# Attention values of the sampled stage: from split fp32r products on 128 weight columns to plain fp32 products on 32 weight columns in four strips

## The reference

```python
def sample_attn(q, k, v, lam, k_past, v_past, rel_bias):
    ...
    s_past = diff_logits(q, q_pos, k_past, jnp.arange(past, dtype=jnp.int32), rel_bias)
    s_new = diff_logits(q, q_pos, k, q_pos, rel_bias)
    w = diff_weights(jnp.concatenate([s_past, s_new], axis=-1), lam).astype(v.dtype)
    return (jnp.einsum('bhqk,bkhe->bqhe', w[..., :past], v_past)
            + jnp.einsum('bhqk,bkhe->bqhe', w[..., past:], v))
```

## Time and profile before

| | |
|---|---|
| median of 3 runs | 2045.65 us (2044.92 to 2045.75) |
| profiled execution, first to last instruction | 2043.6 us |
| difference of the two | 2.05 us |
| TensorE matmul busy | 1993.2 us (98% of the span) |
| VectorE / ScalarE / GpSimd busy | 1375.8 / 998.2 / 131.7 us |
| sampled stage, turns 0 to 8 | about 835 to 1077 us |
| one turn in its middle | 27.5 us |

### The profile page before, as it was taken

The page is one execution under the profiler, slowest core; times in us unless marked ns, Lnnn a source line. Parts: engine busy times, 40 slices in busy tenths (PEclk is TensorE's granted clock), DMA queues, the critical chain, the costliest instruction groups (busy, mean ns, idle before and its releaser), DMA issues. The chain is left out here.

```text
span 2043.6 us, 36009 instructions
## 1 busy us (share of the span) xinstructions
PE 1993.2 (98%) x11888; PEld 1850.2 (91%) x11888; DVE 1375.8 (67%) x2932; ACT 998.2 (49%) x1770; POOL 131.7 (6%) x158
## 2 busy tenths in 40 slices
PE   6999999999999999799999999999999999999998
PEld 6999999999999999688878799999999998989896
DVE  6766776767676767678785376675757474847476
ACT  5756575757565757677874242222313141313133
POOL 0000000000000000145560000000000000000000
PEclk9999999999999999999999999999999999999999
DMA  6411111112121112788873131111112020202012
GB/s 199 144 57 54 57 53 56 53 60 59 50 59 50 59 52 87 261 306 304 316 268 92 38 93 42 53 42 42 52 32 62 22 72 22 72 21 69 6 53 99
DMA packets 167453, 183.26 MB, mean 90 GB/s; under 512 B 11045, under 2 KB 139589, under 8 KB 167349
## 3 DMA queue, kind: packets, MB, share of 16 engines
q1 hardware_dynamic: 166137, 181.24, 27.1%
q10 hardware_dynamic: 1212, 0.81, 0.1%
HBM read 162.82 MB, written 24.46 MB: 92 GB/s over the span
## 5 line engine op out<-in xcount | busy, mean ns | idle before, releaser
L1250 PE MATMUL ps<-h_hi,w_hi 128*128 128x384 f32 (+1 forms) x1152 | 386.7, 336 | 5.0 <-DVEq L967 3.4
L1250 PE MATMUL ps<-h_hi,w_lo 128*128 128x384 f32 (+1 forms) x1152 | 376.5, 327 | 0.0
L1250 PE MATMUL ps<-h_lo,w_hi 128*128 128x384 f32 (+1 forms) x1152 | 376.4, 327 | 0.0
L2456 PE MATMUL ps<-h_hi,f_w_hi 128*128 128x320 f32 (+1 forms) x1136 | 370.7, 326 | 0.8 <-PEq L1579 0.8
L2456 PE MATMUL ps<-h_hi,f_w_lo 128*128 128x320 f32 (+1 forms) x1136 | 370.4, 326 | 0.0
L2456 PE MATMUL ps<-h_lo,f_w_hi 128*128 128x320 f32 (+1 forms) x1136 | 370.2, 326 | 0.0
L2535 ACT ACTIVATE yc<-ps,f_prm 128x384 f32<-128x384 f32 x144 | 93.5, 653 | 560.6 <-PE ps L2456 400.0
L2436 PE MATMUL ps<-d_hi,act 128*128 128x512 f32 x816 | 257.0, 390 | 0.5 <-issue 0.5
L1250 PEld LDWEIGHTS ps<-h_hi,w_hi 128*128 128x128 f32 x1152 | 217.0, 188 | 9.0 <-issue 4.0
L1250 PEld LDWEIGHTS ps<-h_lo,w_hi 128*128 128x128 f32 x1152 | 217.1, 188 | 0.6
L1250 PEld LDWEIGHTS ps<-h_hi,w_lo 128*128 128x128 f32 x1152 | 216.8, 188 | 0.0
(11 more groups left out here) (310 smaller groups left out, 3525.2 us busy)
## 6 DMA issues: line engine op xcount, KB each, us to landing
k<-in_cache_k SPq DMA_DIRECT2D x64, 512.0 KB, 5.9
v_raw<-in_cache_v SPq DMA_DIRECT2D x64, 512.0 KB, 4.7
w_raw<-in_w_in SPq DMA_DIRECT2D x48, 512.0 KB, 4.0
f_raw<-in_w_up SPq DMA_DIRECT2D x48, 512.0 KB, 4.0
f_raw<-in_w_down SPq DMA_DIRECT2D x24, 512.0 KB, 3.5
bias<-bias_tiles_dram SPq DMA_DIRECT2D x8, 576.0 KB, 3.6
merged_dram<-mg SPq DMA_DIRECT2D x8, 544.0 KB, 2.7
ow_raw<-in_w_out SPq DMA_DIRECT2D x8, 512.0 KB, 7.5
```

Source lines behind the costliest of these rows:

```text
L1250: last_ = pe.matmul(bank(s)[:, 0:n], w[:, W_SLOT[g], k, :], x[:, k, off:off + n], start=(k == 0 and i == 0), stop=(k == KT - 1 and i == 2))
L2456: l_ = pe.matmul(ps[:, e % 6, 0:n], w[:, p, k, :], x[:, k, off:off + n], start=(k == 0 and i == 0), stop=(k == KT - 1 and i == 2))
```

## The change

Values and transposed weights are no longer split in the sampled stage. `pt_sb` holds the transposed weights once, in fp32, 64 columns for each page. The matmuls of a page take `v_raw` directly: the half hf of the value columns (heads 4 hf to 4 hf + 3) against the 32 weight columns of these four heads, in plain fp32. The result goes to one of four strips of 32 PSUM partitions of one bank: strip 2 hf + n % 2. The two strips of a half hold the even and the odd pages and are added in the fold. `o2` is one bank instead of two, so `o2s`, the copy and the transposes are half as large. A page waits for its load alone. All splits of value pages, of the new rows and of the transposed weights are gone from ScalarE, VectorE and GpSimd.

```diff
-SPLIT_AT = {2: (0, 1), 3: (2,), 4: (3,), 5: (4, 5), 6: (6,), 7: (7,)}
...
-    o2 = ps[:, 6:8, :].rearrange("p a n -> p (a n)")
-    ptn = ps[:, 6, 0:NS]
+    o2 = ps[:, 6, :]
+    ptn = ps[:, 7, 0:NS]
...
-    pt_both = sb("pt_both", [128, NPAGES + 1, 2, NS], F32R, 158784)
-    o2s = sb("o2s", [128, D], F32, 163392)
+    pt_sb = sb("pt_sb", [128, NPAGES + 1, NS], F32, 158784)
+    o2s = sb("o2s", [128, 512], F32, 163392)
...
+    def strip(hf, n):
+
+        q = 2 * hf + n % 2
+        return o2[32 * q:32 * q + 32, :]
...
-    own_rows = bass.AP(tensor=o2.tensor, offset=o2.offset,
-                       ap=[o2.ap[0], [128 + DEC_T, H], [1, DEC_T], [NS, 2]])
+    def own_rows(hf):
+
+        return bass.AP(tensor=o2.tensor, offset=o2.offset + 64 * hf,
+                       ap=[o2.ap[0], [128 + DEC_T, HH], [1, DEC_T], [32, 2]])
...
-                    if has(b, 1):
-                        for n in splits_of(b).get(h, ()):
-                            if n in POOL_PAGES:
-                                pool.wait_ge(vhi_done, 8 * (b - 1) + n + 1)
-                                pool.tensor_tensor(v_lo[:, n, :], v_raw[:, n, :], v_hi[:, n, :].bitcast(F32),
-                                                   ALU.subtract).then_inc(vplo_done, 1)
...
-                for g in range(H):
+                for g in range(HH):
                     last = pe.transpose(o2[:, 128 * g:128 * (g + 1)], o2s[:, 128 * g:128 * (g + 1)], c.ident[:, :])
...
                 if n == NPAGES:
-                    pe.wait_ge(new_lo, 2)
-                elif n in POOL_PAGES:
-                    pe.wait_ge(vplo_done, pool_low(b, ("v", n)))
+                    pe.wait_ge(vn_in, 32)
                 else:
-                    pe.wait_ge(vlo_done, len(DVE_PAGES) * (b - 1) + DVE_PAGES.index(n) + 1)
+                    pe.wait_ge(v_in[n], 16 * b)
                 for hf in range(2):
                     cols = slice(512 * hf, 512 * (hf + 1))
-                    parts = (v_hi[:, n, cols], v_lo[:, n, cols]) if n < NPAGES else (vn[:, cols],)
-                    for x, v in enumerate(parts):
-                        last = pe.matmul(o2[:, cols], pt_both[:, n, :, :].rearrange("p a n -> p (a n)"), v,
-                                         start=(n == 0 and x == 0), stop=(n == NPAGES - 1 and x == 1))
+                    v = v_raw[:, n, cols] if n < NPAGES else vn_raw[:, cols]
+                    last = pe.matmul(strip(hf, n), pt_sb[:, n, 32 * hf:32 * hf + 32], v,
+                                     start=(n < 2), stop=(n in (NPAGES - 1, NPAGES)))
...
-                            pe.wait_ge(ptlo_done, 2 * b)
+                            pe.wait_ge(pthi_done, 2 * b)
...
-                    if has(b, 1):
-                        for n in splits_of(b).get(h, ()):
-                            act.wait_ge(v_in[n], 16 * b)
-                            act.activation(v_hi[:, n, :], v_raw[:, n, :], ACT.Copy).then_inc(vhi_done, 1)
...
-                    if h == 3 and has(b, 1):
-                        dve.wait_ge(pthi_done, 2 * b)
-                        dve.tensor_tensor(pt_lo[:, 0:NPAGES, :], pt.rearrange("p (n k) -> p n k", n=NPAGES),
-                                          pt_hi[:, 0:NPAGES, :].bitcast(F32), ALU.subtract).then_inc(ptlo_done, 1)
...
-                            dve.wait_ge(vhi_done, 8 * (b - 1) + n + 1)
-                            dve.tensor_tensor(v_lo[:, n, :], v_raw[:, n, :], v_hi[:, n, :].bitcast(F32),
-                                              ALU.subtract).then_inc(vlo_done, 1)
```

More of the change, by code:

```diff
@@ L1396 @@
 HH = H // 2
-SPLIT_AT = {2: (0, 1), 3: (2,), 4: (3,), 5: (4, 5), 6: (6,), 7: (7,)}
 PV_EARLY = {5: (2,)}
 PV_AT = {4: (0, 1), 5: (), 6: (3,), 7: (4,), 8: (5, 6, NPAGES)}
-POOL_PAGES = (1, 3, 5, 7)
-DVE_PAGES = tuple(n for n in range(NPAGES) if n not in POOL_PAGES)
 LAST = DEC_B - 1
-SPLIT_LAST = {1: (0,), 2: (1, 2), 3: (3, 4), 4: (5,), 5: (6,), 7: (7,)}
 OUT_SPLITS = [("m", 0), ("w", 0), ("w", 1), ("w", 2), ("w", 3), ("m", 1), ("w", 4), ("w", 5), ("w", 6), ("w", 7)]
@@ L1406 @@
 OUT_LOW = [x for x in OUT_SPLITS if x[0] == "m" or x[1] >= 4]
-POOL_LAST = [x for h in range(H + 1)
-             for x in [("v", n) for n in SPLIT_AT.get(h, ()) if n in POOL_PAGES]
-             + [x for x in OUT_AT.get(h, ()) if x not in OUT_LOW]]
+POOL_LOW = [x for h in range(H + 1) for x in OUT_AT.get(h, ()) if x not in OUT_LOW]
 def sampled_and_out(nc, sb, sem, ins, outs, c):
@@ L1418, in sampled_and_out @@
     pt = ps[:, 5, :]
-    o2 = ps[:, 6:8, :].rearrange("p a n -> p (a n)")
-    ptn = ps[:, 6, 0:NS]
-    v_hi = sb("sv_hi", [128, NPAGES, D], F32R, 0)
-    v_lo = sb("sv_lo", [128, NPAGES, D], F32R, 32768)
+    o2 = ps[:, 6, :]
+    ptn = ps[:, 7, 0:NS]
     v_raw = sb("v_raw", [128, NPAGES, D], F32, 32768)
@@ L1443, in sampled_and_out @@
     kt_hi, kt_lo = kt[:, 0, :, :], kt[:, 1, :, :]
-    vn = sb("vn", [128, D], F32R, 202752)
     kn = sb("kn", [128, 2, H, NS], F32R, 206848)
@@ L1447, in sampled_and_out @@
     st = c.o_st
-    pt_hi, pt_lo = pt_both[:, :, 0, :], pt_both[:, :, 1, :]
     new_w = P[:, PAST:NKEYS]
-    new_twice = bass.AP(tensor=new_w.tensor, offset=new_w.offset, ap=[new_w.ap[0], [0, 2], [1, DEC_T]])
+    def strip(hf, n):
+        q = 2 * hf + n % 2
+        return o2[32 * q:32 * q + 32, :]
     def strips(part, at):
@@ L1491, in sampled_and_out @@
     c_done = sem("c_done")
-    vhi_done = sem("s_vhi_done")
-    vlo_done = sem("s_vlo_done")
     vplo_done = sem("s_vplo_done")
@@ L1498, in sampled_and_out @@
     pthi_done = sem("pthi_done")
-    ptlo_done = sem("ptlo_done")
     page_done = sem("page_done")
@@ L1547, in bank_of, with pool_low @@
         return 3 if t == 0 else 0 if t % 2 else 2
[L1549 to L1559, removed]
+    def pool_low(what):
+        return POOL_LOW.index(what) + 1
     def all_turns(eng, body):
@@ L1602, in new_weights @@
                     pool.sem_inc(settled, 1)
-                    pool.tensor_copy(p_new[:, :, bass.ds(DEC_T * (b - 2), DEC_T)], zeros[:, :, :]).then_inc(s_fill, 1)
+                    pool.tensor_copy(p_new[:, 0, bass.ds(DEC_T * (b - 2), DEC_T)], zeros[:, 0, :]).then_inc(s_fill, 1)
                 pool.wait_ge(exp_done, b)
                 pool.sem_inc(settled, 1)
-                pool.tensor_copy(p_new[:, :, bass.ds(DEC_T * (b - 1), DEC_T)], new_twice).then_inc(s_fill, 1)
+                pool.tensor_copy(p_new[:, 0, bass.ds(DEC_T * (b - 1), DEC_T)], new_w).then_inc(s_fill, 1)
             def weights_low(h):
@@ L1824, in out_tile @@
                     if t == 0 and k < 4:
-                        pe.wait_ge(vplo_done, pool_low(LAST, ("w", k)))
+                        pe.wait_ge(vplo_done, pool_low(("w", k)))
                     elif t == 0:
@@ L1927, in body @@
                         act.wait_ge(pt_done, b)
-                        act.activation(pt_hi[:, 0:NPAGES, :], pt.rearrange("p (n k) -> p n k", n=NPAGES), ACT.Copy)\
+                        act.activation(pt_sb[:, 0:NPAGES, :], pt.rearrange("p (n k) -> p n k", n=NPAGES), ACT.Copy)\
                            .then_inc(pthi_done, 1)
-                        act.activation(pt_hi[:, NPAGES, :], ptn, ACT.Copy).then_inc(pthi_done, 1)
+                        act.activation(pt_sb[:, NPAGES, :], ptn, ACT.Copy).then_inc(pthi_done, 1)
                     if h == 0 and at_start(b):
@@ L1941, in body @@
                             queries(b + 1, 0)
-                    if h == HH + 1 and isinstance(b, int) and b == 1:
-                        act.wait_ge(vn_in, 32)
-                        act.activation(vn[:, :], vn_raw[:, :], ACT.Copy).then_inc(new_hi, 1)
                     if h == 1 and has(b, 2):
@@ L2056, in fold_rows @@
                 dve.wait_ge(ot_done, b + 1)
-                dve.reduce_sum(oT[:, :, bass.ds(DEC_T * b, DEC_T)], own_rows, mybir.AxisListType.X)                   .then_inc(ots_done, 1)
+                for hf in range(2):
+                    last = dve.reduce_sum(oT[:, HH * hf:HH * (hf + 1), bass.ds(DEC_T * b, DEC_T)], own_rows(hf),
+                                          mybir.AxisListType.X)
+                last.then_inc(ots_done, 1)
             def split_out(what, i):
@@ L2082, in body @@
                         keys(b, h)
-                    if h == 3 and has(b, 1):
-                        dve.wait_ge(pthi_done, 2 * b)
-                        dve.tensor_tensor(pt_lo[:, 0:NPAGES, :], pt.rearrange("p (n k) -> p n k", n=NPAGES),
-                                          pt_hi[:, 0:NPAGES, :].bitcast(F32), ALU.subtract).then_inc(ptlo_done, 1)
-                        dve.tensor_tensor(pt_lo[:, NPAGES, :], ptn, pt_hi[:, NPAGES, :].bitcast(F32),
-                                          ALU.subtract).then_inc(ptlo_done, 1)
                     if at_start(b) and h == 0:
@@ L2096, in body @@
                         queries(b, HH)
[L2097 to L2100, removed]
                     if h == HH and has(b, 0):
@@ L2728 @@
```

(4 more changed lines are left out.)

## The result

The changed kernel takes 2022.15 us, the kernel before 2045.29 us in the same comparison. (The 2022.15 is the median of four runs: 2020.24, 2021.65, 2022.65 and one of 4954.44 us that stands alone; the median of the other three is 2021.65.) The ratio is 0.9882, 95% interval 0.9866 to 0.9898: 23 us faster. I had forecast 2058 us and slower, with 2018 to 2108 us as the range. The rival "four at once" had 2020 us.

The account below looks back on a forecast made before the run. TensorE's stream, busy 98%, was taken as the bound. A turn: 2.19 + 1.0 - 0.97 = +2.2 us, seven +15.5; with +0.2 - 3.0 - 0.3, +12.4 on 2045.65 gave 2058 us, range 2018 to 2108.

Parts of the forecast that it names:

- four at once: Rival: value matmuls in the four strips run free of each other; -2.6 us a turn, 2020 us; chance 0.27.
- What bounds it: Whole kernel: TensorE, busy 98% of the span, is nearly the bound; its idle time in five middle turns is for `kt_lo`.
- The cost of a record: Value matmuls: each plain fp32 matmul of 512 columns is two trace records of 0.44 us, 0.88 us in all.
- the groups of 4, 2, 2, 2 and 8: A turn's adjacent value matmuls: pages 0 and 1; page 2; page 3; page 4; pages 5, 6, new rows, 7.
- part 1: Value matmuls: m adjacent ones take (m + 1) x 0.44 us, 23 slots or 10.12 us a turn, 2.19 us more.
- part 2: TensorE entering and leaving strips: five groups a turn at 0.09 us each way, taken as 1.0 us, bounds 0.5 to 1.5.
- Part 3: Work taken from ScalarE, VectorE and GpSimd: 0.54 us for splits and 0.43 for `copy_o2`, 0.97 us a turn saved.
- My own sign that the size is wrong: Profile after: the size is wrong if a 32-column record is not 0.44 us or TensorE still waits as long for `kt_lo`.
- The ends: Turn 7 saves 3.0 us, the wait for the first output weights 0.3; turn 8 costs 0.2 more.
- None at once: Rival: column strips run one after the other; +7.9 us a turn, 2106 us; chance 0.23.
- The clock: Rival: strips use a quarter of the array and the granted clock drops once each turn; 2070 us; chance 0.08.

Follow-up runs that it names:

- e1: The changed kernel with all 18 value matmuls of a sequence sent to strip 0; 2103.36 us, ratio 1.028.
- e3: The changed kernel, but in turn 8 alone all nine pages of the first half are multiplied before the second half; 2025.13 us.
- e4: The kernel before, without strips, with value splits done for the first sequence alone and high parts multiplied twice later; 2036.34 us, ratio 0.9953.
- e5: The changed kernel with the value splits put back as work without use, TensorE waiting for them as before; 2040.44 us, ratio 0.9972.
- e6: The changed kernel with pages 2 and 3 multiplied together at h = 6, page 4 with 5, 6 and the new rows at h = 8; 2020.67 us.
- e7: The changed kernel with VectorE's maximum moved after `keys(b, 1)` of the next turn and the exponentials to h = 2; 2018.70 us, ratio 0.9871.
- e11: e7 with VectorE's subtraction for the second half of the queries also moved behind kt_lo of head 2; 2018.80 us, ratio 0.9871.

## Why the prediction was wrong, point by point

- **What bounds it** was right: TensorE's stream, with waits for `kt_lo`.
- **The cost of a record** (0.44 us) was right: 0.43 in e1. So were the groups of 4, 2, 2, 2 and 8.
- **The step that failed** is in part 1: "I take that order to hold here. Then the two records of one fp32 matmul, which share a strip, must follow each other; the second of them and the first record of the next strip can run together". I applied the order to records. The runs show otherwise: a waiting second record does not hold up the next strip, four matmuls start together, and each strip runs its two records. Time for a group is the fullest strip's records times 0.43, not (m + 1) x 0.44. For a turn that is 12 rounds, not 23 slots: 5.8 us with the visits (going into the strips and out again, part 2), where I had 10.12 + 1.0. The values got 2.1 us a turn cheaper; the sum had them 3.2 us dearer. The page "TensorE: Matmul & The Clock Gate" of the Trainium skill, Part 3, "The mechanism", says that matmuls keep their order in start and end; e3, and turn 8 of the changed kernel, show a later matmul passing an earlier one that waits for its strip, so the trace does not agree in that point., the evidence that I had, held no case in which order and free strips disagreed.
- **Going in and out** was mis-sized: 0.98 - 2 x 0.43 = 0.12 us a visit, 0.6 us a turn, not 1.0. It hardly matters.
- **Freed engines.** Part 3 gave 0.97 us a turn. e4, without the smaller `copy_o2`, shows 0.46 of the 0.54 meant for the splits. In the changed kernel the waits before head 3 went, as said, but 0.85 us at the start of the turn is new: the last group is short now (1.85 us), and VectorE has the sum and the maximum to do before `kt_lo`. I had looked at what a slower TensorE would hide, not at what a faster one uncovers. Values 2.1, splits 0.46 and my 0.43 for `copy_o2`, which no run measures by itself, would make 3.0 us a turn; 2.2 came. My own sign that the size is wrong, TensorE waiting for `kt_lo` as long as before, came true (4.7 us against 4.6).
- **The ends** were right: the distance from turn 7 to 8 fell by 5.8 us, 3.6 more than a middle turn (3.3 said for turn 7 and the first weights), with no stretch at half clock left in it (from 1030 to 1062 us the granted clock is 1.00, before it was 0.95). The stretch from turn 8's `C` product to the end of the kernel fell from 982.4 to 978.6 us (3.75, the rival's figure for turn 8; my own sum had turn 8 at +0.2).
- **The rivals.** "Four at once" had the mechanism and nearly the size, 25.4 us less in sum. That the span fell by 25.2 is in part luck: the seven distances between turns gave 20.3 us and turn 8 3.75, together 24.0, and 1.15 us come from before turn 1's `C` product (863.21 against 864.36 us), where the change does next to nothing; in the other traces this moment lies between 862.8 and 866.6. I gave it 0.27, because I took an order seen between plain matmuls as proof about the inside of a matmul. "None at once" is e1 (2106 said for it, 2103 measured with all in one strip). "The clock" did not happen.

## What to carry to other kernels

Plain fp32 with at most 32 weight columns, spread over four strips of output partitions, ran at the price of one fp32r pass a matmul (4.41 us for 18 of 512 columns, 0.245 each), and needed no splitting of the moving operand. Put matmuls for different strips next to each other: with two for one strip in a row next to nothing was lost (4.48 us against 4.41), with more of them in line the other strips stood idle (7.02). Before calling two savings more than additive, look at the turns one by one: here they gave 5 and 9 us alone and 23 together, but by the trace of e5 7 of the 9 us in between came from one small subtraction that in three turns started 0.01 us too late. And a wait that is taken away can come back elsewhere: in e6, e7 and e11 it did, and a middle turn gained 0.4 us at most.

## What the runs showed of the hardware that I had not expected

- The first records of four plain fp32 matmuls in four strips start together (within 0.02 us), ahead of the second record of the first (8 loads within 0.16 us, then mostly four each 0.43 us).
- Matmuls pass a waiting one when their strip is free, but not without limit: 7.02, 4.48 and 4.41 us for the same 18 matmuls in three orders.
- A small VectorE subtraction (64 x 32) that starts 0.008 us after a GpSimd subtraction of 128 x 1024 takes 2.42 us and ends with it; started up to 0.009 us before or 0.004 us after, it takes 0.19 (e5, and the kernel before).
